# h_hi and h_lo computed directly from x and the gains, without a gained temporary, in a two-layer decoder trunk

## Chip, cores and metric

The kernel runs on one core of one Trainium2 chip. The metric is the device time of one execution in microseconds; shorter is better. The kernel before takes 2354.09 us, the median of 3 runs (2353.06 to 2355.17).

## What is computed

A trunk of two layers over 512 tokens of width 1024, all in float32. Each layer is half a SwiGLU block, a mixer with memory attention beside it, and another half SwiGLU block. Each part begins with an RMS norm. Cut to what matters:

```python
def rmsnorm(x, g):
    y = x * lax.rsqrt(jnp.mean(x * x, axis=-1, keepdims=True) + EPS)
    return y * g

for i in range(2):
    x = x + 0.5 * swiglu_ffn(rmsnorm(x, ffn1_norm[i]), ffn1_w_in[i], ffn1_w_out[i])
    h = rmsnorm(x, mix_norm[i])
    z = h @ w_in                                   # HGRN2 in layer 0, chunked gMLP in layer 1
    x = x + concat(mixer(z), memory_attention(z, mem_k, mem_v)) @ w_out
    x = x + 0.5 * swiglu_ffn(rmsnorm(x, ffn2_norm[i]), ffn2_w_in[i], ffn2_w_out[i])
return rmsnorm(x, final_norm)
```

## The kernel before, in words

x lies feature-major: 8 blocks of 128 features by 512 tokens. Every product of two float32 matrices is made of three TensorE (PE) matmuls: each operand is split into a high half, rounded to the type fp32r, and a low half, the operand less its high half. The PE computes high by high (L1093), high by low (L1094) and low by high (L1095). `unit` is one such product: one block of 128 output features, over 8 blocks of the contraction (24 matmuls of 512 columns) or, in the last third of an FFN's second matrix, over 6 (18 matmuls).

Weights come in units too. Four lanes of one buffer are used in turn. SyncE loads a lane (`raw`) once the PE is through with the unit that used it four units before; ScalarE (ACT) rounds it into `w_hi` (`hi`, L1528); VectorE (DVE) forms `w_lo` = raw - w_hi in place (`lo`, L1255). Both are issued two units ahead of the one being multiplied (`ahead`).

A phase is one weight matrix: first the memory's K and V for both layers (32 short units, "kv"), then for each layer `ffn_in`, `ffn_out`, the mixer's in and out, `ffn_in`, `ffn_out`. The last `ffn_out` is done by other code (`Final`).

Between phases stands h. In a phase whose name ends in `_out`, the four last units of each half give four new blocks of x. `take(g)` on DVE adds the PE's bank into x (L1478). Then, still in `take`, `gained` multiplies the block by the norm's gain, one value per partition, into a temporary (L1314); ACT's `h_top` rounds the temporary into `h_hi` (L1550); DVE's `h_rest` subtracts that from the temporary into `h_lo` (L1318). The factor 1/rms is applied later, to the results (`rstd`). GpSimd (POOL) squares each block of x (L1751) and adds it to a running sum (L1753). The first unit of the next phase reads h block by block and waits for each `h_lo`; behind it the PE multiplies the sum of squares by ones (L1159), from which DVE and ACT form `rstd` (L1363, L1586, L1365), which every later result needs.

In the kv phase the blocks of h for the first `ffn_in` are formed in the same three steps, one block per four units: `h_block` (the multiplication, DVE), `h_top` and `h_rest`. ACT also moves V out of PSUM there (`take_v`, L1560), and POOL stores it to DRAM (L1765).

Every engine works its queue strictly in the order of the code, so what stands ahead of an instruction in its queue can hold it. The order in the last four units (r == nr - 1) of an `_out` phase is, for step g:

```python
# DVE                                         # ACT
if g: take(g - 1)  # add, gained, h_rest      if g >= 1: take(g - 1)  # h_top
lo(next but one lane)                         hi(next but one lane)
# and after the four steps: take(3)
```

Of the kernel before, what the change touches and what calls it, by code (L numbers as in the profile page):

```python
# [30 lines left out]
ACT = mybir.ActivationFunctionType  # L31
# [5 lines left out]
DB = D // P  # L37
# [16 lines left out]
LANES = 4  # L54
# [30 lines left out]
def hybrid_trunk(nc, a, out):  # L85
# [34 lines left out]
    with ExitStack() as ctx:  # L120
# [5 lines left out]
        def sem(name):  # L126
            if name not in sems:
                sems[name] = ctx.enter_context(nc.semaphore(name))
            return sems[name]
# [50 lines left out]
        def f32(ap):  # L180
            return ap.bitcast(F32)
# [13 lines left out]
        def ahead(q, j):  # L195

            return (q, j + 2) if j + 2 < LANES else (q + 1, j - 2)

        def blocks_ahead(kind, r, g):

            rows = OUT_ROWS[kind]
            return rows[(r + (g >= 2)) % len(rows)][2]
# [2 lines left out]
        w_hi_ready, w_lo_ready = sem("w_hi_ready"), sem("w_lo_ready")  # L205
        unit_done = sem("unit_done")
        acc_read = sem("acc_read")
        xg_ready, h_hi_ready, h_lo_ready = sem("xg_ready"), sem("h_hi_ready"), sem("h_lo_ready")
        sq_ready, sq_sum_ready = sem("sq_ready"), sem("sq_sum_ready")
        ss_done, var_ready, std_ready, rstd_ready = (sem("ss_done"), sem("var_ready"), sem("std_ready"),  # L210
                                                     sem("rstd_ready"))
# [1040 lines left out]
        def _(dve):  # L1252
            def lo(q, j, nkb=KU):
                dve.wait_ge(w_hi_ready, LANES * q + j + 1)
                dve.tensor_tensor(lane_of(w_lo, q, j)[:, 0:nkb], lane_of(raw, q, j)[:, 0:nkb], f32(lane_of(w_hi, q, j)[:, 0:nkb]),  # L1255
                                  ALU.subtract).then_inc(w_lo_ready, 1)
# [51 lines left out]
                dve.tensor_scalar(small[:, 32:40], small[:, 24:32], -1.0, 1.0, ALU.mult, ALU.add).then_inc(sem("lb_step"), 1)  # L1308
                dve.wait_ge(sem("lb_step"), 7)

            def gained(s, m_, t):

                g = GAINS[s] + m_
                dve.tensor_scalar(t, x[:, m_, :], vecs[:, bass.ds(g, 1)], None, ALU.mult).then_inc(xg_ready, 1)  # L1314

            def h_rest(s, m_, t):
                dve.wait_ge(h_hi_ready, DB * s + m_ + 1)
                dve.tensor_tensor(h_lo[:, m_, :], t, f32(h_hi[:, m_, :]), ALU.subtract).then_inc(h_lo_ready, 1)  # L1318


            def kv_quad(it):
                first, turn = it == 0, kv_turn_of(it)

                def take(j):
                    if KV_QUADS[it] == "k":
                        dve.wait_ge(unit_done, LANES * it + j + 1)
                        if turn:
                            dve.wait_ge(sem(f"k_stored{j}"), 16 * turn)
                        dve.tensor_tensor(tmp[:, j, 0:MEM], acc[j][:, 0:MEM], rstd[:, 0:MEM], ALU.mult).then_inc(acc_read, 1)
                    if 2 <= LANES * it + j < DB + 2:  # L1330
                        take_x(LANES * it + j - 2)

                def h_block(m):
                    dve.wait_ge(sem("x_ready"), m + 1)
                    if m:
                        dve.wait_ge(h_lo_ready, m)
                    gained(0, m, tmp[:, 4, :])
                for j in range(LANES):
                    if first and j == 1:
                        lo(0, 3)  # L1340
                    if j:
                        take(j - 1)
                    if j == 1 and it:
                        h_block(it - 1)
                    if j == 2 and it:
                        h_rest(0, it - 1, tmp[:, 4, :])
                    if j == 2 and it == DB - 1:
                        h_block(it)
                    if j == 3 and it == DB - 1:
                        h_rest(0, it, tmp[:, 4, :])  # L1350
                    if not (first and j < 2):
                        lo(*ahead(it, j))
                take(3)
# [15 lines left out]
            for i, (kind, ph) in enumerate(phases):  # L1369
# [96 lines left out]
                elif ph is final.ph:  # L1466
                    final.vector(dve, lo)
                else:
                    rows = OUT_ROWS[kind]
                    nr = len(rows)  # L1470
                    scale = 0.5 if kind == "ffn_out" else 1.0
                    s += 1

                    def body(it, beside=None):
                        def take(g):
                            m_, t = LANES * it + g, tmp[:, 4 + g % 2, :]
                            dve.wait_ge(unit_done, LANES * (ph.q0 + nr * it + nr - 1) + g + 1)
                            dve.scalar_tensor_tensor(x[:, m_, :], acc[g][:], scale, x[:, m_, :], ALU.mult,  # L1478
                                                     ALU.add).then_inc(acc_read, 1)
                            dve.wait_ge(acc_read, ph.g0 + m_ + 1)  # L1480
                            gained(s, m_, t)
                            h_rest(s, m_, t)
                        for r in range(nr):
                            for g in range(LANES):
                                if beside:
                                    beside(LANES * r + g)
                                if r == nr - 1 and g:
                                    take(g - 1)
                                lo(*ahead(ph.q0 + nr * it + r, g), blocks_ahead(kind, r, g))
                        take(3)  # L1490
                    if kind == "hgrn_out":
                        hg = mixes[i - 1][1]

                        def beside(u):
                            if u < LANES:
                                hg.vector(dve, HEADS, u, False, True, True)
                            if u == LANES:
                                hg.vector(dve, HEADS + 1, 0, False, False, True)
                        body(0, beside)
                        body(1)  # L1500
                    elif kind == "gmlp_out":
                        gm = mixes[i - 1][1]

                        def beside(u):
                            if u < LANES:
                                gm.norm_vector(dve, 3, u)
                            if u == 0:
                                gm.u_vector(dve, 3, 3)
                                gm.mix_vector(dve, 2, 3)
                                gm.rest_vector(dve, 2, 3)  # L1510
                            if 1 <= u <= LANES:
                                gm.mix_vector(dve, 3, u - 1)
                                gm.rest_vector(dve, 3, u - 1)
                        body(0, beside)
                        body(1)
                    else:
                        loop(dve, 0, 2, body)
                        n_ffn += 1
# [3 lines left out]
        def _(act):  # L1522
# [22 lines left out]
            act.wait_ge(sem("mem_var"), 1)  # L1545
            act.activation(small[:, 60:62], small[:, 60:62], ACT.Sqrt).then_inc(sem("mem_std"), 1)

            def h_top(s, m_, t):
                act.wait_ge(xg_ready, DB * s + m_ + 1)
                act.activation(h_hi[:, m_, :], t, ACT.Copy).then_inc(h_hi_ready, 1)  # L1550

            def take_v(it, p):

# [9 lines left out]
            for it, kind in enumerate(KV_QUADS):  # L1563
                for j in range(LANES):
                    if it == 0 and j == 1:
                        hi(0, 3)
                    if it == 2 and j == 0:
                        act.wait_ge(sem("lb_shifted"), 3)
                        act.activation(small[:, 72:96], small[:, 72:96], ACT.Exp).then_inc(sem("lb_exp"), 1)
                        act.wait_ge(sem("mem_rstd"), 1)  # L1570
                    if j == 2 and it == DB - 1:
                        h_top(0, it, tmp[:, 4, :])
                    if j == 1:
                        if it:
                            h_top(0, it - 1, tmp[:, 4, :])
                        if it and KV_QUADS[it - 1] == "v":
                            take_v(it - 1, 1)
                    if j == 3 and kind == "v":
                        take_v(it, 0)
                    if not (it == 0 and j == 1):  # L1580
                        hi(*ahead(it, j))
# [7 lines left out]
            for i, (kind, ph) in enumerate(phases):  # L1589
# [85 lines left out]
                else:  # L1675
# [2 lines left out]

                    def body(it, beside=None):
                        def take(g):  # L1680
                            h_top(s, LANES * it + g, tmp[:, 4 + g % 2, :])
                        for r in range(nr):
                            for g in range(LANES):
                                if beside:
                                    beside(LANES * r + g)
                                if r == nr - 1 and g >= 1:
                                    take(g - 1)
                                hi(*ahead(ph.q0 + nr * it + r, g), blocks_ahead(kind, r, g))
                        take(3)
                    if kind == "hgrn_out":  # L1690
                        hg = mixes[i - 1][1]
# [151 lines left out]
```

## Time and profile before

| what | value |
|---|---|
| median of 3 runs | 2354.09 us |
| the profiled execution's own time | 2353.23 us |
| span of its trace | 2351.5 us |
| PE busy | 2328.8 us, 99% |
| DVE busy | 1233.5 us, 52% |
| ACT busy | 764.4 us, 33% |
| POOL busy | 264.5 us, 11% |
| PE's share of the chain that ended last | 92% |
| mean DMA rate | 100 GB/s |

The profile is of one execution. Its span runs from the first to the last instruction; 1.7 us of the execution's time lie around it. In the timeline the start of an instruction is given in us from the span's start, then its length; brackets show how long its engine had been idle and what released it. A matmul's length is modelled and overlaps the next one; the distance between starts is what a matmul costs.

### The profile page before, as it was taken

The numbers are of one execution on the slowest core, as the hardware profiler recorded it, in microseconds if no ns is written. First come the engines' busy times: TensorE is split into PE (matmuls) and PEld (weight loads), VectorE is DVE, ScalarE is ACT, GpSimd is POOL, SyncE is SP. The second block draws the span as 40 slices with busy tenths as digits, with TensorE's granted clock in tenths as the row PEclk, the third lists the DMA queues.
The fourth block names the chain that finished last, engine by engine and source line by source line (L and its number), as shares of the span: only waits on it lengthen the run. The fifth ranks groups of instructions, "written<-read, shape, count | busy, mean of one in ns | idle before, by whom it ended". The sixth has DMA issues, their size and how long they took to land.

```text
span 2351.5 us, 29800 instructions
## 1 busy us (share of the span) xinstructions
PE 2328.8 (99%) x11040; PEld 1947.6 (83%) x11040; DVE 1233.5 (52%) x1467; ACT 764.4 (33%) x1045; POOL 264.5 (11%) x236
## 2 busy tenths in 40 slices
PE   9999999999999999999999999999999999999998
PEld 9988888878888888888878888888888888888887
DVE  6654443467888654444445444336437644444422
ACT  4432222244445322222222222224433222222322
POOL 3400001111333420000110000120001212000000
PEclk9999999999999999999999999999999999999999
DMA  7733333332222333333333333333232233333322
GB/s 235 215 98 95 93 97 99 95 104 69 72 71 80 99 97 92 97 98 98 98 90 90 98 98 98 97 92 107 72 99 85 86 98 99 99 98 97 92 95 92
DMA packets 400693, 234.35 MB, mean 100 GB/s; under 512 B 7692, under 2 KB 386672, under 8 KB 400624
## 3 DMA queue, kind: packets, MB, share of 16 engines
q1 hardware_dynamic: 397328, 223.37, 32.1%
q0 software_dynamic: 3280, 10.02, 1.2%
q8 instruction: 47, 0.77, 0.1%
q14 instruction: 22, 0.18, 0.0%
q10 hardware_dynamic: 16, 0.00, 0.0%
HBM read 227.07 MB, written 6.29 MB: 99 GB/s over the span
## 4 chain that ended last, share of the span: by engine, by line
PE 92%; DVE 4%; ACT 2%; issue 1%; DMA 1%; POOL 0%; DVEq 0%; ACTq 0%; SPq 0%; POOLq 0%
PE acc L1093 26%; PE acc L1094 26%; PE acc L1095 26%; PE acc L847 1%; PE acc L846 1%; PE acc L848 1%; ACT w_hi L1528 1%; DVE w_lo L1255 1%; PE acc L262 1%; PE acc L264 1%; PE acc L263 1%; PE mix L264 1%; PE mix L262 1%; PE mix L263 1%; DMA raw<-in_mem_w_kv_dram 1%
## 5 line engine op out<-in xcount | busy, mean ns | idle before, releaser
L1255 DVE TENSOR_TENSOR w_lo<-raw,w_hi 128x1024 fp32r<-128x1024 f32 (+1 forms) x422 | 544.9, 1294 | 636.2 <-ACT w_hi L1528 623.1
L1093 PE MATMUL acc<-h_hi,w_hi 128*128 128x512 f32 x1920 | 756.0, 394 | 7.6 <-DVE h_lo L1318 5.3
L1094 PE MATMUL acc<-h_lo,w_hi 128*128 128x512 f32 x1920 | 748.5, 390 | 0.0
L1095 PE MATMUL acc<-h_hi,w_lo 128*128 128x512 f32 x1920 | 748.4, 390 | 0.0
L1528 ACT ACTIVATE w_hi<-raw 128x1024 fp32r<-128x1024 f32 (+1 forms) x422 | 436.4, 1038 | 341.7 <-DMA raw<-in_ffn_w_out_dram 219.6
L1093 PEld LDWEIGHTS acc<-h_hi,w_hi 128*128 128x128 f32 x1920 | 361.5, 188 | 84.4 <-DVE h_lo L1318 6.6
L1094 PEld LDWEIGHTS acc<-h_lo,w_hi 128*128 128x128 f32 x1920 | 361.5, 188 | 75.4 <-issue 2.0
L1095 PEld LDWEIGHTS acc<-h_hi,w_lo 128*128 128x128 f32 x1920 | 361.2, 188 | 75.4
L1093 PE MATMUL acc<-act_hi,w_hi 128*128 128x512 f32 (+1 forms) x976 | 367.6, 377 | 1.9 <-DVE w_lo L1255 1.2
L1095 PE MATMUL acc<-act_hi,w_lo 128*128 128x512 f32 (+1 forms) x976 | 365.7, 375 | 0.0
L1094 PE MATMUL acc<-act_lo,w_hi 128*128 128x512 f32 (+1 forms) x976 | 365.7, 375 | 0.0
L1381 DVE TENSOR_TENSOR tmp<-acc,rstd 128x512 f32<-128x512 f32 x176 | 121.7, 691 | 202.2 <-PE acc L1095 201.9
L1093 PEld LDWEIGHTS acc<-act_hi,w_hi 128*128 128x128 f32 x976 | 183.2, 188 | 36.0 <-DVE w_lo L1255 1.4
L1095 PEld LDWEIGHTS acc<-act_hi,w_lo 128*128 128x128 f32 x976 | 183.3, 188 | 33.2
L1094 PEld LDWEIGHTS acc<-act_lo,w_hi 128*128 128x128 f32 x976 | 183.5, 188 | 32.7
L1600 ACT ACTIVATE act_hi<-tmp 128x512 f32 (+1 forms) x88 | 55.6, 632 | 404.3 <-DVE tmp L1387 404.3
L1751 POOL TENSOR_TENSOR sq<-x 128x512 f32 (+1 forms) x48 | 57.6, 1201 | 1131.3 <-DVE x L1478 1130.7
L1596 ACT ACTIVATE tmp<-tmp 128x512 f32<-128x512 f32 x88 | 55.6, 632 | 255.5 <-DVE tmp L1381 255.5
L1550 ACT ACTIVATE h_hi<-tmp 128x512 fp32r<-128x512 f32 (+1 forms) x48 | 30.4, 632 | 200.7 <-DVE tmp L1314 200.7
L1392 DVE TENSOR_TENSOR act_lo<-tmp,act_hi 128x512 f32 (+1 forms) x88 | 60.6, 689 | 40.1 <-ACT act_hi L1600 40.1
L1753 POOL TENSOR_TENSOR sq<-sq 128x512 f32<-128x512 f32 x48 | 78.3, 1631 | 3.8
L1387 DVE TENSOR_TENSOR tmp<-tmp 128x512 f32<-128x512 f32 x88 | 60.9, 692 | 10.7
(243 smaller groups left out, 1895.0 us busy)
## 6 DMA issues: line engine op xcount, KB each, us to landing
raw<-in_ffn_w_in_dram SPq DMA_DIRECT2D x176, 512.0 KB, 3.7
raw<-in_ffn_w_out_dram SPq DMA_DIRECT2D x70, 512.0 KB, 3.4
raw<-in_hgrn_w_in_dram SPq DMA_DIRECT2D x40, 512.0 KB, 3.7
raw<-in_gmlp_w_in_dram SPq DMA_DIRECT2D x40, 512.0 KB, 3.6
raw<-in_mem_w_kv_dram SPq DMA_DIRECT2D x32, 512.0 KB, 4.4
raw<-in_gmlp_w_out_dram SPq DMA_DIRECT2D x24, 512.0 KB, 3.4
raw<-in_ffn_w_out_dram SPq DMA_DIRECT2D x24, 384.0 KB, 3.0
raw<-in_hgrn_w_out_dram SPq DMA_DIRECT2D x16, 512.0 KB, 3.4
```

Source lines behind the costliest of these rows:

```text
L1093: pe.matmul(bank, top[:, i, :], hi, start=(start and i == 0), stop=False)
L1094: pe.matmul(bank, top[:, i, :], lo, start=False, stop=False)
L1095: m = pe.matmul(bank, rest[:, i, :], hi, start=False, stop=(stop and i == last))
L1255: dve.tensor_tensor(lane_of(w_lo, q, j)[:, 0:nkb], lane_of(raw, q, j)[:, 0:nkb], f32(lane_of(w_hi, q, j)[:, 0:nkb]), ALU.subtract).then_in ...
L1381: dve.tensor_tensor(tmp[:, j, :], acc[j][:], rstd[:], ALU.mult).then_inc(acc_read, 1)
L1387: dve.tensor_tensor(tmp[:, j, :], tmp[:, j, :], tmp[:, j - 1, :], ALU.mult).then_inc(prod_done, 1)
L1392: dve.tensor_tensor(act_lo[:, f, :], tmp[:, j, :], f32(act_hi[:, f, :]), ALU.subtract).then_inc(act_lo_ready, 1)
L1528: act.activation(lane_of(w_hi, q, j)[:, 0:nkb], lane_of(raw, q, j)[:, 0:nkb], ACT.Copy).then_inc(w_hi_ready, 1)
L1596: act.activation(tmp[:, j, :], tmp[:, j, :], ACT.Silu).then_inc(silu_done, 1)
L1600: act.activation(act_hi[:, 2 * it + j // 2, :], tmp[:, j, :], ACT.Copy).then_inc(act_hi_ready, 1)
L1751: pool.tensor_tensor(sq_one, x[:, m_, :], x[:, m_, :], ALU.mult).then_inc(sq_ready, 1)
L1753: pool.tensor_tensor(sq_sum, sq_sum, sq_one, ALU.add).then_inc(sq_sum_ready, 1)
```

## The change

The multiplication by the gain into a temporary is removed with the semaphore `xg_ready`. ACT forms `h_hi` straight from x, with the gain as the activation's per-partition scale; DVE forms `h_lo` = x * gain - h_hi in one `scalar_tensor_tensor`. ACT's wait is now for x itself (`acc_read`, or `x_ready` in the kv phase). In the last four units of an `_out` phase the order on both engines changes: DVE adds into x, then splits the weights of the lane two ahead, then forms `h_lo`; ACT rounds those weights before it forms `h_hi`.

```diff
-            def gained(s, m_, t):
+            def h_rest(s, m_):
 
                 g = GAINS[s] + m_
-                dve.tensor_scalar(t, x[:, m_, :], vecs[:, bass.ds(g, 1)], None, ALU.mult).then_inc(xg_ready, 1)
-
-            def h_rest(s, m_, t):
                 dve.wait_ge(h_hi_ready, DB * s + m_ + 1)
-                dve.tensor_tensor(h_lo[:, m_, :], t, f32(h_hi[:, m_, :]), ALU.subtract).then_inc(h_lo_ready, 1)
-
+                dve.scalar_tensor_tensor(h_lo[:, m_, :], x[:, m_, :], vecs[:, bass.ds(g, 1)], f32(h_hi[:, m_, :]),
+                                         ALU.mult, ALU.subtract).then_inc(h_lo_ready, 1)
...
-                def h_block(m):
-                    dve.wait_ge(sem("x_ready"), m + 1)
-                    if m:
-                        dve.wait_ge(h_lo_ready, m)
-                    gained(0, m, tmp[:, 4, :])
...
-                    if j == 1 and it:
-                        h_block(it - 1)
                     if j == 2 and it:
-                        h_rest(0, it - 1, tmp[:, 4, :])
-                    if j == 2 and it == DB - 1:
-                        h_block(it)
+                        h_rest(0, it - 1)
                     if j == 3 and it == DB - 1:
-                        h_rest(0, it, tmp[:, 4, :])
+                        h_rest(0, it)
...
                         def take(g):
-                            m_, t = LANES * it + g, tmp[:, 4 + g % 2, :]
+                            m_ = LANES * it + g
...
-                            dve.wait_ge(acc_read, ph.g0 + m_ + 1)
-                            gained(s, m_, t)
-                            h_rest(s, m_, t)
...
                                 lo(*ahead(ph.q0 + nr * it + r, g), blocks_ahead(kind, r, g))
+                                if r == nr - 1 and g:
+                                    h_rest(s, LANES * it + g - 1)
                         take(3)
+                        h_rest(s, LANES * it + 3)
...
-            def h_top(s, m_, t):
-                act.wait_ge(xg_ready, DB * s + m_ + 1)
-                act.activation(h_hi[:, m_, :], t, ACT.Copy).then_inc(h_hi_ready, 1)
+            def h_top(s, m_, source, count):
+
+                g = GAINS[s] + m_
+                act.wait_ge(source, count)
+                act.activation(h_hi[:, m_, :], x[:, m_, :], ACT.Copy, scale=vecs[:, bass.ds(g, 1)]).then_inc(h_hi_ready, 1)
...
                     if j == 2 and it == DB - 1:
-                        h_top(0, it, tmp[:, 4, :])
+                        h_top(0, it, sem("x_ready"), it + 1)
                     if j == 1:
                         if it:
-                            h_top(0, it - 1, tmp[:, 4, :])
+                            if it == 1:
+                                act.wait_ge(sem("vecs_ready"), 2)
+                            h_top(0, it - 1, sem("x_ready"), it)
...
                         def take(g):
-                            h_top(s, LANES * it + g, tmp[:, 4 + g % 2, :])
+                            h_top(s, LANES * it + g, acc_read, ph.g0 + LANES * it + g + 1)
                         for r in range(nr):
                             for g in range(LANES):
                                 if beside:
                                     beside(LANES * r + g)
+                                hi(*ahead(ph.q0 + nr * it + r, g), blocks_ahead(kind, r, g))
                                 if r == nr - 1 and g >= 1:
                                     take(g - 1)
-                                hi(*ahead(ph.q0 + nr * it + r, g), blocks_ahead(kind, r, g))
                         take(3)
```

## Rows read from the trace of the kernel before

**Rows 1.** The page, part 1: busy us, share of the span, instructions
```profile
PE 2328.8 (99%) x11040; PEld 1947.6 (83%) x11040; DVE 1233.5 (52%) x1467; ACT 764.4 (33%) x1045; POOL 264.5 (11%) x236
```

**Rows 2.** The waits of PE: total us, times, longest
```profile
PE acc L1093 <- DVE h_lo L1318: 5.3, 3, 2.2
PE acc L1093 <- DVE w_lo L1255: 3.4, 4, 2.3
```

**Rows 3.** Timeline of PE at four of its idle stretches
```profile
70.96 0.36 PE L1093 MATMUL acc<-act_hi,w_hi 128*128 128x256 f32 x1 [0.36 <-DVE w_lo L1255]
...
109.81 0.77 PE L1093 MATMUL acc<-h_hi,w_hi 128*128 128x512 f32 x1 [2.27 <-DVE w_lo L1255]
...
1228.41 0.50 PE L1093 MATMUL acc<-h_hi,w_hi 128*128 128x512 f32 x1 [2.08 <-DVE h_lo L1318]
...
1591.32 0.50 PE L1093 MATMUL acc<-h_hi,w_hi 128*128 128x512 f32 x1 [1.05 <-DVE h_lo L1318]
...
1592.46 1.12 PE L1159 MATMUL mix<-sq,ones 128*128 128x512 f32 x2 [0.18 <-POOL sq L1753]
```

**Rows 4.** Timeline of PE at the end of layer 0's first ffn_out
```profile
471.46 0.39 PE L1093 MATMUL acc<-h_hi,w_hi 128*128 128x512 f32 x1
...
476.00 0.39 PE L1095 MATMUL acc<-h_hi,w_lo 128*128 128x512 f32 x1
478.60 0.79 PE L1093 MATMUL acc<-h_hi,w_hi 128*128 128x512 f32 x1 [2.21 <-DVE h_lo L1318]
```

**Rows 5.** Stretches: length, busy us by engine, granted PE clock, DMA share, GB/s
```profile
109.80:113.20 3.40, 3.39 (x8) 2.73 (x9) 1.50 (x2) 3.13 (x5) 2.71 (x4) 0.50 0.63 218
...
575.30:578.70 3.40, 1.41 (x12) 1.17 (x11) 2.64 (x3) 2.93 (x5) 2.17 (x2) 1.00 0.53 154
```

**Rows 6.** Timeline of DVE, same place as rows 4
```profile
469.58 0.68 DVE L1478 SCALAR_TENSOR_TENSOR x<-acc,x 128x512 f32 x1
470.41 1.37 DVE L1314 TENSOR_SCALAR tmp<-x,vecs 128x512 f32 x1
472.68 0.80 DVE L1318 TENSOR_TENSOR h_lo<-tmp,h_hi 128x512 f32 x1 [0.90 <-ACT h_hi L1550]
473.53 1.23 DVE L1255 TENSOR_TENSOR w_lo<-raw,w_hi 128x1024 fp32r<-128x1024 f32 x1
474.67 0.68 DVE L1478 SCALAR_TENSOR_TENSOR x<-acc,x 128x512 f32 x1
```

**Rows 7.** Timeline of POOL, same place
```profile
470.46 1.04 POOL L1751 TENSOR_TENSOR sq<-x 128x512 f32 x1 [2.62 <-DVE x L1478]
471.57 1.36 POOL L1753 TENSOR_TENSOR sq<-sq 128x512 f32<-128x512 f32 x1
```

**Rows 8.** Timeline of DVE, then POOL, near the end of kv
```profile
102.47 1.93 DVE L1255 TENSOR_TENSOR w_lo<-raw,w_hi 128x1024 fp32r<-128x1024 f32 x1 [2.37 <-ACT w_hi L1528]
104.32 1.77 DVE L1318 TENSOR_TENSOR h_lo<-tmp,h_hi 128x512 fp32r<-128x512 f32 x1
...
103.39 2.16 POOL L1753 TENSOR_TENSOR sq<-sq 128x512 f32<-128x512 f32 x1
```

**Rows 9.** Timeline of ACT, end of kv
```profile
106.72 0.63 ACT L1550 ACTIVATE h_hi<-tmp 128x512 fp32r<-128x512 f32 x1 [4.29 <-DVE tmp L1314]
...
109.87 0.83 ACT L1560 ACTIVATE tmp<-acc,small 128x256 f32<-128x256 f32 x2
```

**Rows 10.** Groups by form: busy us, mean ns, idle before
```profile
L861 ACT ACTIVATE work<-acc,small 128x512 f32<-128x512 f32 x16 | 10.8, 688 | 11.6 <-PE acc L848 11.6
```

**Rows 11.** Timeline of SyncE, and DMA issues of the page, part 6
```profile
463.72 0.37 SPq L973 DMA_DIRECT2D raw<-in_hgrn_w_in_dram  x1
...
raw<-in_hgrn_w_in_dram SPq DMA_DIRECT2D x40, 512.0 KB, 3.7
```

**Rows 12.** Timeline of DVE at the start of the first ffn_in
```profile
117.75 1.23 DVE L1255 TENSOR_TENSOR w_lo<-raw,w_hi 128x1024 fp32r<-128x1024 f32 x1 [6.46 <-DMA v_scratch<-tmp]
...
126.00 1.23 DVE L1255 TENSOR_TENSOR w_lo<-raw,w_hi 128x1024 fp32r<-128x1024 f32 x1 [1.65 <-ACT w_hi L1528]
```

More of the change, by code:

```diff
@@ L207, in hybrid_trunk @@
         acc_read = sem("acc_read")
-        xg_ready, h_hi_ready, h_lo_ready = sem("xg_ready"), sem("h_hi_ready"), sem("h_lo_ready")
+        h_hi_ready, h_lo_ready = sem("h_hi_ready"), sem("h_lo_ready")
         sq_ready, sq_sum_ready = sem("sq_ready"), sem("sq_sum_ready")
```

## The prediction

> **What bounds the kernel now.** The page comes first: the PE is busy 99% of the span, and DVE, ACT and POOL have room [rows 1]. A faster DVE is therefore worth nothing on average; only PE's idle time can be won. The list of PE's waits says how little that is: 5.3 us for `h_lo` in three places, 3.4 us for `w_lo` in four, the longest 2.3 [rows 2]. PE's timeline puts the long ones where phases meet. I call them A (end of kv, idle 2.27 us for `w_lo`), B (end of layer 0's first `ffn_out`, 2.21 for `h_lo`), C (layer 0's second, 2.08) and D (layer 1's first, 1.05) [rows 3, 4]. A fifth, G, is 0.36 us inside kv.
>
> Idle is not the whole price. In the 3.4 us after A the granted clock is 0.50, and the matmuls run at the 1.2 GHz level instead of 2.4; the same happens once after B and once after C (three stretches, one shown), but not after D, nor around 575 us, where the PE was idle for 2.0 us for another reason and the row shows 1.00 [rows 5]. Each such stretch costs half its length, 1.7 us.
>
> So between matmul starts, at 0.227 us each (471.46 to 476.00 are 20 steps), B lost 478.60 - 476.23 = 2.4 us, plus 1.7 for the clock. C lost 2.2 + 1.7. (A modelled end overlaps the next start, so the idle shown at B, 2.21, is 0.16 short of the loss; I add that at the others.) A lost 2.4 + 1.7. D lost 1.2 of idle, 0.3 in its slow restart (1592.46 - 1591.32 less three matmuls and the 0.18), and that 0.18 before the squares' matmul [rows 3, 4]. G lost 0.4. Altogether 14.2 us, 0.6% of the kernel. That is the ceiling.
>
> **Why B, C and D stall.** The last units of `ffn_out` have 18 matmuls, 4.1 us. DVE's step from one add to the next is 474.67 - 469.58 = 5.1 us [rows 6]: add 0.7, gain 1.4, wait for ACT 0.9, `h_lo` 0.8, `w_lo` 1.2. It falls 1 us behind per unit. The fourth unit's result exists at about 471.7 (the next unit starts at 471.46 [rows 4]), but its add starts at 474.67 and `h_lo` comes 3.9 us later, at 478.5. The PE needs that block 21 matmuls after 471.46, at 476.2. `hgrn_out` and `gmlp_out` end in units of 24 matmuls, 5.4 us, more than DVE's 5.1, and no stall shows there.
>
> **The parts of the change.**
>
> Removed: 48 gain multiplications. Alone one takes 0.49 us, but beside POOL's square (470.46 to 471.50) it took 1.37 and ended 0.3 after POOL did [rows 6, 7]: a blocked instruction. That part of 1.4 us per step goes, with the wait of 0.15 before it, and with it the semaphore hop to ACT.
>
> Added on ACT: a scale read from a column. The trace has it in L861, 0.69 us from PSUM [rows 10]; without it `h_hi` takes 0.63 [rows 9]. I take 0.63 and keep 0.69 as the other end; it is hidden behind DVE's `w_lo` either way.
>
> Added on DVE: `h_lo` as scalar_tensor_tensor with two SBUF tensors. The nearest rows are L1478 with one operand in PSUM, 0.68, and the subtraction it replaces, 0.69 to 0.80 [rows 6]. I take 0.7. The upper end is 1.77, that subtraction beside POOL at 104.32 [rows 8].
>
> This upper end matters, since the removed instruction leaves two-tensor instructions alone beside POOL. At 102 to 106 us they alternate: `w_lo` 1.93, POOL's add 2.16 instead of 1.36, `h_lo` 1.77, each waiting for the one before [rows 7, 8]. The Trainium skill, "SBUF — State Buffer", section "Who interferes with whom", has a rule for it: a DVE instruction with two SBUF inputs and a GpSimd instruction that reads SBUF exclude each other for their whole length, and whoever comes first wins. By that rule, the trace agrees at 104.32, and a fused `h_lo` can be blocked no less than the old one. Without any blocking a step would be 0.7 + 1.2 + 0.7 = 2.6 us.
>
> I reckon the blocking in. x is ready at T + 0.7. In the new order `w_lo` is next in DVE's queue, if `w_hi` is there; POOL wakes 0.2 us later (469.58 + 0.68 against 470.46 [rows 6, 7]), so `w_lo` should win: 1.2, then POOL's square 1.04, then `h_lo` 0.7. Step: 3.6 us, under 4.1. ACT forms `h_hi` meanwhile. If POOL wins every time: 0.85 + 1.04 + 1.1 + 1.36 + 0.7 = 5.0, hardly better than now.
>
> Is `w_hi` there? ACT now rounds the weights ahead of `h_hi`. The lane for step 3 is asked for at 463.72 and lands 3.7 later, at 467.4 [rows 11]; rounding takes at most 1.2, as the same block's `w_lo` [rows 6], so 468.5 or so, and that step's add ends at 467.8 + 0.7 = 468.5. It is a close race in steps 2 and 3 and clear in step 1. With one race lost, lag is below 1 us: add 471.9 to 473.4 at worst, `h_lo` of the last block 474.3 to 475.2. Needed: 476.2. The stall is gone, and with the idle the slow clock. What is late next? The sum of squares: POOL's square and add follow the last x and end near 475.5 to 476.5, and the PE asks at 471.46 + 5.45 = 476.9. It fits, narrowly. Gain: B 4.1, C 3.9, D 1.7.
>
> A. ACT's `h_hi` of the last block stands ahead of the rounding of the lane that A waits for, and was itself idle 4.29 us for the gain multiplication, which stood behind the two blocked DVE instructions [rows 8, 9]. Now it needs only x, long ready. That lane is asked for when the last kv unit but three is done. Kv's last units have 256 columns, so 2.8 us each, half of 5.4; PE's idle began at 109.81 - 2.27 = 107.5 [rows 3], so the load starts near 99. It lands 3.7 later [rows 11], is rounded by 104 and has its `w_lo` by 105.3, before the PE's 107.4. But another chain follows: `w_lo` of the third `ffn_in` unit waits for V's last store (6.46 us idle), and the fourth unit's ends at 126.00 + 1.23 = 127.2 [rows 12]. The store begins after `take_v`, at 109.87 [rows 9], held by ACT's queue; now its unit is done at 107.5 and it can start at 107.6, so this chain moves forward only 2.2 us, to 125.0. The PE, 2.4 us earlier and at full clock, wants that fourth unit at 107.4 + 3 x 5.45 + 0.9 = 124.6 (0.9 is L1159, 1.12 less its overlap [rows 3]). New stall 0.4 to 0.5 us. Gain of A: 4.1 - 0.5 = 3.6.
>
> G. `w_lo` came late through the same ACT queue: 0.4.
>
> Sum: 4.1 + 3.9 + 1.7 + 3.6 + 0.4 = 13.7 us. The profiled execution took 2353.23 (span 2351.5 and 1.7 around it), giving 2339.5; the median of the runs is 0.9 higher, giving 2340.4.
>
> Costed at nothing: the changed order in the first halves of the `_out` phases and in `hgrn_out` and `gmlp_out`. Its cover is the PE's 5.4 us per unit against a step of at most 5.0; without that cover it would cost up to 0.5 us in each of two places.
>
> **Rivals.**
>
> *POOL wins the races.* Steps of 5.0 us leave the last add 2.7 us late at 474.6; `h_lo` then takes 0.7 + 1.2 + 0.7 and ends at 477.2, a stall of 1.0. For it: the gain multiplication lost that race at 470.41 by 0.05 us. Against: `w_lo` does not wait for the add. B and C keep 1.0 each, D keeps most of 1.2; one idle microsecond brought no slow clock at D. Gain 13.7 - 3.2 = 10.5, or 7.1 if the clock falls all the same: 2344 to 2347.
>
> *The clock or A takes some back.* The idle stretch at 575 us is 2.0 long and stays; C's was 2.08 and did lower the clock. Falling there or at the fourth unit of A costs 1.7 each: 2342 to 2344.
>
> *A new wait takes the old one's place.* The PE waits for the sum of squares instead of `h_lo`, since POOL is the loser of the races that DVE wins. Three squares and adds, each delayed by 1.2, would end the sum 2 us late, and the slow clock stays: 2350 to 2354, no change. Against it: POOL works 2.4 of 4.1 us per unit.
>
> *Slower: a late weight load now holds h.* ACT's queue puts `h_hi` behind a DMA. After the landing, rounding, `h_hi`, a blocked wait and `h_lo` take 3.8 us, so block 6 is there at 471.3 and needed at 475.5. From a load of 8 us upwards each us is a us of PE time, and beyond 10.5 us the place is worse than before. To be slower by over 0.2% it would take loads of about 12 us at B, C and D together. The row's 3.7 speaks against it.
>
> **How the numbers follow.** Forecast 0.60; POOL wins 0.13; clock or A 0.13; new wait 0.09; slower 0.05. Predicted time 2340.4. The forecast's own range is 2338 to 2342.5 (the ceiling of 14.2, the spread of the runs, the half microseconds of A and of the races). To leave out no more than 2 in 10 the range takes in the next two cases: 2337.5 to 2347. A change of under 0.2% (4.7 us) can't be told from none here: faster 0.86, same 0.09, slower 0.05.
>
> **What would show it.** PE's waits: `h_lo` gone or under 1 us, `w_lo` under 1 us; the granted clock 1.00 behind A, B and C; starts of the adds at the end of `ffn_out` 4.1 us apart; `h_lo` lengths between 0.7 and 1.8; at A a new wait at the fourth `ffn_in` unit. I am wrong if the adds stay 5 us apart, if L1159 waits for POOL by over 1 us, or if a slow stretch of the clock turns up elsewhere.

## The result: 14.9 us faster, and the profile after

The changed kernel takes 2339.16 us, the median of 5 runs (2338.49 to 2340.8), against 2354.09 before (5 runs, 2352.48 to 2355.17). The ratio is 0.9938, with a 95% interval of 0.9925 to 0.9952. The forecast was 2340.4.

The profiled execution took 2339.09 us with a span of 2337.3, 14.2 less than before. The first part of its page, and then the list of PE's waits (total us, times, longest; two of 0.3 and 0.2 left out), answer to [rows 1, 2]:

```profile
PE 2321.8 (99%) x11040; PEld 1944.8 (83%) x11040; DVE 1207.4 (52%) x1419; ACT 772.6 (33%) x1045; POOL 278.2 (12%) x236
```

```profile
PE mix L580 <- POOL work L767: 2.0, 1, 2.0
PE acc L1051 <- POOL small L1716: 1.9, 1, 1.9
PE acc L1093 <- DVE act_lo L1267: 1.8, 1, 1.8
PE mix L455 <- DVE act_hi L418: 1.6, 1, 1.6
PE acc L1137 <- DVE w_lo L1255: 0.3, 1, 0.3
```

The 5.3 us for `h_lo` are gone altogether. Of the 3.4 for `w_lo`, A (2.3) and G (0.4) are gone, and 0.3 came new in another place. The remaining 0.8 were two waits at 14.6 and 18.4 us, at the kernel's start, which the change doesn't touch. DVE has 48 instructions less.

What still holds the PE lies elsewhere. The 1.8 us for `act_lo` stand at the kernel's start, at 11 us, and were 0.5 in the profile before. The PE was through with its transposes 1.0 us earlier than before, and what it waits for came 0.3 us later. Behind this wait the granted clock was 0.51 for 3.4 us, a slow stretch that the profile before does not have (1.00 there in the same stretch):

```profile
11.07 0.36 PE L1093 MATMUL acc<-act_hi,w_hi 128*128 128x256 f32 x1 [1.83 <-DVE act_lo L1267]
...
12.10:15.50 3.40, 3.40 (x18) 3.40 (x17) 2.77 (x5) 3.37 (x6) 0.00 (x0) 0.51 1.02 420
```

It cost nothing that lasted: matmul for matmul, the changed kernel was 0.8 us behind the one before at 16 us and level with it at 35 us.

Set side by side matmul by matmul, the two traces drift apart for good in four places: 4.1 us at A, 4.1 at B, 3.9 at C, 1.7 at D. The remaining 0.3 lies before A. The timeline of DVE in the changed kernel, at the place of [rows 6], shows how:

```profile
459.19 0.69 DVE L1466 SCALAR_TENSOR_TENSOR x<-acc,x 128x512 f32 x1 [1.07 <-PE acc L1095]
459.91 1.23 DVE L1255 TENSOR_TENSOR w_lo<-raw,w_hi 128x1024 fp32r<-128x1024 f32 x1
461.05 1.53 DVE L1315 SCALAR_TENSOR_TENSOR h_lo<-x,vecs,h_hi  x1
463.27 0.69 DVE L1466 SCALAR_TENSOR_TENSOR x<-acc,x 128x512 f32 x1 [0.70 <-PE acc L1095]
464.10 1.23 DVE L1255 TENSOR_TENSOR w_lo<-raw,w_hi 128x1024 fp32r<-128x1024 f32 x1
465.24 1.53 DVE L1315 SCALAR_TENSOR_TENSOR h_lo<-x,vecs,h_hi  x1
467.36 0.69 DVE L1466 SCALAR_TENSOR_TENSOR x<-acc,x 128x512 f32 x1 [0.58 <-PE acc L1095]
469.18 0.75 DVE L1315 SCALAR_TENSOR_TENSOR h_lo<-x,vecs,h_hi  x1 [1.13 <-ACT h_hi L1540]
```

The adds start 4.1 us apart instead of 5.1, and before each DVE is idle, waiting for the PE: it is the PE that sets the pace. POOL's timeline at the same place, with the last two matmul groups of PE behind it:

```profile
464.16 2.07 POOL L1743 TENSOR_TENSOR sq<-x 128x512 f32 x1 [0.43 <-DVE x L1466]
466.30 1.62 POOL L1745 TENSOR_TENSOR sq<-sq 128x512 f32<-128x512 f32 x1
468.24 1.04 POOL L1743 TENSOR_TENSOR sq<-x 128x512 f32 x1 [0.31 <-DVE x L1466]
469.36 1.72 POOL L1745 TENSOR_TENSOR sq<-sq 128x512 f32<-128x512 f32 x1
```

```profile
467.03 0.39 PE L1093 MATMUL acc<-h_hi,w_hi 128*128 128x512 f32 x1
...
472.24 0.40 PE L1095 MATMUL acc<-h_hi,w_lo 128*128 128x512 f32 x1
472.47 1.02 PE L1159 MATMUL mix<-sq,ones 128*128 128x512 f32 x2
```

The blocking has changed sides ("blocked" means here that an instruction has started but ends only some time after another engine's). POOL's square, alone 1.04 us, takes 2.07 where `w_lo` was first; `h_lo` then waits for the square and takes 1.53 instead of 0.75. The last `h_lo` ends at 469.93; the PE would want it 21 matmuls after 467.03, at 471.8. The sum of squares is ready at 471.1, wanted at 472.5.

At C it went less smoothly. DVE's timeline and, behind it, POOL's:

```profile
1205.19 0.69 DVE L1466 SCALAR_TENSOR_TENSOR x<-acc,x 128x512 f32 x1 [1.07 <-PE acc L1095]
1206.16 2.04 DVE L1255 TENSOR_TENSOR w_lo<-raw,w_hi 128x1024 fp32r<-128x1024 f32 x1 [0.28 <-ACT w_hi L1516]
1208.12 1.78 DVE L1315 SCALAR_TENSOR_TENSOR h_lo<-x,vecs,h_hi  x1
1209.82 0.68 DVE L1466 SCALAR_TENSOR_TENSOR x<-acc,x 128x512 f32 x1
```

```profile
1206.07 1.04 POOL L1743 TENSOR_TENSOR sq<-x 128x512 f32 x1 [0.81 <-DVE x L1466]
```

`w_hi` came late, POOL's square began 0.1 us before `w_lo`, and the step took 4.6 us. The next one took 3.5, and DVE was waiting for the PE again. One lost step of 4.6 is covered.

The stretches behind A and around B of the changed kernel (length, busy us by engine, granted clock, DMA share, GB/s) answer to [rows 5]:

```profile
107.10:113.50 6.40, 6.40 (x29) 4.95 (x28) 1.23 (x1) 3.83 (x5) 3.40 (x4) 1.00 0.68 213
467.00:474.00 7.00, 7.00 (x30) 5.45 (x29) 4.08 (x4) 2.96 (x3) 6.02 (x6) 1.00 0.38 104
```

The PE is busy throughout at a granted clock of 1.00.

### The profile page after: what moved, and what is told of

Read it like the earlier page. It is cut to its first block, busy times and chain, and to the rows that moved or that the text cites. A ratio compares the mean times of both kernels' runs of the same rounds, so it can differ in the third digit from the quotient of the medians.

```text
span 2337.3 us, 29722 instructions
## 1 busy us (share of the span) xinstructions
PE 2321.8 (99%) x11040; PEld 1944.8 (83%) x11040; DVE 1207.4 (52%) x1419; ACT 772.6 (33%) x1045; POOL 278.2 (12%) x236
## 4 chain that ended last, share of the span: by engine, by line
PE 94%; DVE 3%; ACT 1%; POOL 0%; DMA 0%; issue 0%; SPq 0%; ACTq 0%; DVEq 0%; POOLq 0%
PE acc L1093 26%; PE acc L1095 26%; PE acc L1094 26%; PE acc L846 1%; PE acc L848 1%; PE acc L847 1%; PE acc L262 1%; PE acc L264 1%; PE acc L263 1%; PE mix L263 1%; PE mix L262 1%; PE mix L264 1%; DVE w_lo L1255 1%; PE acc L1137 1%; PE mix L913 1%; PE acc L1138 1%
## 5 line engine op out<-in xcount | busy, mean ns | idle before, releaser
L1255 DVE TENSOR_TENSOR w_lo<-raw,w_hi 128x1024 fp32r<-128x1024 f32 (+1 forms) x422 | 534.8, 1269 | 643.7 <-ACT w_hi L1516 632.6
L1743 POOL TENSOR_TENSOR sq<-x 128x512 f32 (+1 forms) x48 | 70.5, 1469 | 1106.7 <-DVE x L1466 1105.1
L1466 DVE SCALAR_TENSOR_TENSOR x<-acc,x 128x512 f32 (+1 forms) x40 | 27.6, 691 | 79.6 <-PE acc L1095 79.6
```

The costliest lines, as they stand in the source:

```text
L1743: pool.tensor_tensor(sq_one, x[:, m_, :], x[:, m_, :], ALU.mult).then_inc(sq_ready, 1)
```

## The experiments

The rival theories were these: the stalls went because DVE has one instruction less, blocked or not; because POOL no longer stretches it; or because of the new order, which fills the wait for ACT with other work. And, for the size of the gain, whether the slow clock belongs to each stall.

**One phase at a time.** `kv_only` takes from the change what stands in the kv phase, `out_only` the rest.

```diff
# kv_only: h_block and its gained() removed; for layer 0's first ffn_in
-  h_top(0, it - 1, tmp[:, 4, :])
+  h_top_x(0, it - 1, sem("x_ready"), it)
-  h_rest(0, it - 1, tmp[:, 4, :])
+  h_rest_x(0, it - 1)
# out_only: the same two functions, and the new order, in the _out phases alone
```

> The change in the kv phase alone; all _out phases as before. Theory (the gain multiplication and ACT's queue held the first ffn_in's weights; 2.4 us of idle plus 1.7 of slow clock): 4.2 us faster than before, about 2350; C, B and D keep their 4.1, 3.9 and 1.7. Rival (the gain came from the order in the _out phases only, and A moved with chance): no difference beyond 1 us.

> The change in the _out phases alone; kv as before. Theory: 9.7 us faster than before, about 2344.5, A keeps its idle of 2.3 us and the slow clock behind it. Rival (the parts are not additive, one slow stretch of the clock moves elsewhere): 7 to 8 us, with a slow stretch at a new place.

Measured: `kv_only` 2346.86 us (7 runs), ratio 0.997 (0.9959 to 0.9981), 6.9 us under the 2353.8 of before on the same chip; `out_only` 2345.78 (5 runs), ratio 0.9964 (0.995 to 0.9977), 8.0 us. Both parts help and their sum, 14.9, is what the whole gives. But the division is not the expected 4.2 and 9.7. In `kv_only`'s trace A is gone, C is as before, and B kept its idle, but no slow stretch lies behind it. That missing stretch is 1.7 us of gain which the edit did not aim at. In `out_only`'s trace A kept its 2.27 us of idle, without a slow stretch; one lies behind the stall at 572 us instead, which had none before. That the two gains add up to the whole is therefore partly luck: each depends on which of the stalls left in it brought a slow stretch.

**Fusion without the order.**

```diff
# fuse_only: the changed kernel, last four units
-  lo(next but one lane)
   if r == nr - 1 and g: h_rest(s, LANES * it + g - 1)
+  lo(next but one lane)
# and on ACT
-  hi(next but one lane)
   if r == nr - 1 and g >= 1: take(g - 1)      # h_top
+  hi(next but one lane)
```

> h_hi and h_lo from x as in the changed kernel, everywhere, but with the old order in the last four units: DVE add, h_lo, weights; ACT h_hi ahead of the weights. Theory (blocking by POOL counts, order does the rest): a step of 4.1 to 5.0 us, the add of the fourth unit up to 2.7 us late, a stall of 0 to 1 us at each ffn_out; 2339 to 2345. Rival (the removed instruction alone is enough): step 4.1, no stall, 2339, the same as the changed kernel.

Measured: 2340.02 us (2339.47 to 2341.65), ratio 0.994 (0.9927 to 0.9954): within 1 us of the changed kernel. The step, though, is not 4.1. DVE's timeline in `fuse_only`:

```profile
465.10 0.68 DVE L1466 SCALAR_TENSOR_TENSOR x<-acc,x 128x512 f32 x1
466.90 0.75 DVE L1315 SCALAR_TENSOR_TENSOR h_lo<-x,vecs,h_hi  x1 [1.13 <-ACT h_hi L1540]
467.72 2.17 DVE L1255 TENSOR_TENSOR w_lo<-raw,w_hi 128x1024 fp32r<-128x1024 f32 x1
469.81 0.68 DVE L1466 SCALAR_TENSOR_TENSOR x<-acc,x 128x512 f32 x1
```

It is 4.7 us, DVE still lags behind the PE, and waits 1.1 us for ACT in every step. The lag just fits into the cover that the next phase's first unit gives `h_lo`. What no longer fits is the sum of squares. Its last add on POOL and PE's L1159 in `fuse_only`:

```profile
471.80 1.72 POOL L1745 TENSOR_TENSOR sq<-sq 128x512 f32<-128x512 f32 x1
```

```profile
473.03 0.39 PE L1095 MATMUL acc<-h_hi,w_lo 128*128 128x512 f32 x1
473.57 1.13 PE L1159 MATMUL mix<-sq,ones 128*128 128x512 f32 x2
```

The add ends at 473.52 and L1159 starts at 473.57, 0.54 after the matmul before it instead of 0.23. That is 0.3 us, and 0.35 to 0.4 in all at each of B, C and D: about 1.1 us, the size of the difference between the two medians, but smaller than what these runs can tell apart.

**Order without the fusion.**

```diff
# order_only: the kernel before, last four units
   take(g - 1)       # add and gained, without h_rest
   lo(next but one lane)
+  h_rest(s, LANES * it + g - 1, tmp[:, 4 + (g - 1) % 2, :])
# and on ACT hi() ahead of h_top()
```

> Before, with only the new order in the last four units of the _out phases: DVE add, gain multiplication, weights, h_lo; ACT weights ahead of h_hi. kv as before. Theory (the wait of 0.9 us for ACT is filled with the weights' split, the gain multiplication stays blocked at 1.4): step 4.1 to 4.5 us, B, C and D mostly gone, 2345 to 2349. Rival (only the removed instruction helps): adds stay 5 us apart, 2354.

Measured: 2350.43 us (11 runs, 2349.04 to 2353.74), ratio 0.9988 (0.9979 to 0.9997): 3.4 us faster, less than my theory had. DVE's timeline:

```profile
465.14 1.37 DVE L1314 TENSOR_SCALAR tmp<-x,vecs 128x512 f32 x1
466.43 2.31 DVE L1255 TENSOR_TENSOR w_lo<-raw,w_hi 128x1024 fp32r<-128x1024 f32 x1
468.66 0.68 DVE L1318 TENSOR_TENSOR h_lo<-tmp,h_hi 128x512 f32 x1
469.26 0.68 DVE L1478 SCALAR_TENSOR_TENSOR x<-acc,x 128x512 f32 x1
```

```profile
466.30 1.36 POOL L1755 TENSOR_TENSOR sq<-sq 128x512 f32<-128x512 f32 x1
```

The wait of 0.9 for ACT is filled, but `w_lo` now meets POOL's add (the second fence), which used to run beside that wait, and takes 2.31 instead of 1.23. The adds stay 4.95 us apart; B keeps 1.79 us of idle. I had forgotten that an empty stretch of DVE was where POOL worked unhindered.

The 3.4 us overstate what the order does. PE's waits for `h_lo` fell only from 5.3 to 4.0 us. The larger part of the 3.8 us between the two profiled executions is the clock: this trace has a slow stretch behind B alone, so two fewer than before, 3.4 us. One of the two is A's, where the idle is 2.28 us and the edit changes nothing.

**Which engine's order.**

```diff
# fuse_act_order: the changed kernel with DVE's old order and ACT's new one
-  lo(next but one lane)
   if r == nr - 1 and g: h_rest(s, LANES * it + g - 1)
+  lo(next but one lane)
```

> The changed kernel with DVE's old order (add, h_lo, weights) and ACT's new one (weights ahead of h_hi). Theory: DVE's h_lo now waits for ACT, which rounds weights first when they land late; the order on DVE matters, step 4.5 to 5, 2340 to 2345. Rival (ACT's order is what matters): as the changed kernel, 2339.

Measured: 2340.72 us (2338.59 to 2341.44), ratio 0.9946 (0.9932 to 0.9959). Its step is 4.7 us like `fuse_only`'s, and it keeps the same 0.4 us at B, C and D. So what little the order gives comes from DVE's side; ACT's alone gives nothing that the trace shows. The medians can't tell these kernels apart, and DVE's new order with ACT's old one was not tried.

**Without POOL's work.** The same edit in the kernel before and in the changed one:

```diff
-  pool.tensor_tensor(sq_one, x[:, m_, :], x[:, m_, :], ALU.mult).then_inc(sq_ready, 1)
-  pool.wait_ge(sq_ready, DB * s + m_ + 1)
-  pool.tensor_tensor(sq_sum, sq_sum, sq_one, ALU.add).then_inc(sq_sum_ready, 1)
+  pool.sem_inc(sq_ready, 1)            # in the _out phases only
+  pool.sem_inc(sq_sum_ready, 1)
```

> Before, with POOL's squares and adds of the _out phases left out (only semaphores are raised; the sum is a constant, so the later norms are not computed). If POOL's use of SBUF is what stretches DVE's instructions: the gain multiplication takes 0.49 us everywhere, h_lo 0.69, a step is 4.1 to 4.2 us, and B, C and D vanish: about 2344.5. If the stretch has another cause, or the number of instructions alone counts: steps stay at 5.1 and the time at 2354.

> The changed kernel with the same work left out. If blocking by POOL is hidden in the changed order: h_lo takes 0.74 us in the _out phases instead of 1.5, and the time stays at 2339 within 1 us. If POOL still costs PE time somewhere: faster by more than 1 us.

Measured: 2345.02 us for before (ratio 0.9964, 0.995 to 0.9977) and 2341.05 for the changed one (0.9945, 0.9931 to 0.9959; 2339.03 to 2341.41). In the first, every gain multiplication takes 0.49 us. DVE's timeline of it, a step of 4.2:

```profile
465.39 0.69 DVE L1478 SCALAR_TENSOR_TENSOR x<-acc,x 128x512 f32 x1
466.23 0.49 DVE L1314 TENSOR_SCALAR tmp<-x,vecs 128x512 f32 x1
467.63 0.69 DVE L1318 TENSOR_TENSOR h_lo<-tmp,h_hi 128x512 f32 x1 [0.91 <-ACT h_hi L1550]
468.47 1.22 DVE L1255 TENSOR_TENSOR w_lo<-raw,w_hi 128x1024 fp32r<-128x1024 f32 x1 [0.15 <-ACT w_hi L1528]
```

B, C and D vanish with nothing of the change made. So POOL's square and add were what made the gain multiplication dear, and removing either them or it is enough. In the changed kernel `h_lo` falls from a median of 1.44 to 0.75 us and the time does not fall: there the blocking is covered. (Its median is even 1.9 us above the changed kernel's, which ran at another time; the two profiled executions, 2339.31 and 2339.09, are 0.2 apart.)

**The clock.** Since the slow stretches had not stayed with their stalls, the kernel before was profiled twice more, and the two halves of the change once more each.

> The kernel before once more, for a second profile. If the slow clock follows each idle stretch of over 2.05 us by rule: stretches at A, B and C again, none at 575. If it is partly chance: another set of places, and a time that differs by 1.7 us for each one more or less, with the idle stretches themselves the same.

> The kernel before, a third profile. By rule: slow stretches of the clock behind A, B and C, none at 575, as in the first. By chance: another set, the idle stretches the same.

> The change in the kv phase alone, a second profile. Its first had 2.3 us of idle at B and no slow stretch there, but one at C. By rule: the same again. By chance: another set.

> The change in the _out phases alone, a second profile. Its first had A's idle of 2.4 us without a slow stretch, and one behind the 2.0 us at 570. By rule: the same again. By chance: another set.

Measured, one execution each: 2352.84, 2356.54, 2347.69 and 2345.66 us. PE's idle at C in `before_again` and in `before_third`, and the stretches around it (the clock is the figure in front of the last two):

```profile
1229.63 0.50 PE L1093 MATMUL acc<-h_hi,w_hi 128*128 128x512 f32 x1 [2.08 <-DVE h_lo L1318]
...
1227.00:1235.00 8.00, 5.92 (x25) 4.21 (x24) 5.71 (x5) 4.77 (x5) 2.48 (x3) 1.00 0.24 66
```

```profile
1231.77 0.50 PE L1093 MATMUL acc<-h_hi,w_hi 128*128 128x512 f32 x1 [2.08 <-DVE h_lo L1318]
...
580.20:583.60 3.40, 3.40 (x13) 2.92 (x12) 3.23 (x3) 2.56 (x4) 1.29 (x1) 0.51 0.02 6
1229.00:1237.00 8.00, 5.92 (x18) 3.75 (x17) 4.55 (x5) 4.31 (x5) 2.61 (x3) 0.79 0.22 66
```

The row from 580.20 lies behind the stall of 2.0 us near 575 us. The idle stretches repeat to 0.02 us; the slow ones do not. 2.08 us of idle at C brought none in `before_again` and one in the other two profiles; the 2.0 us at 575, which I had taken for harmless, brought one in `before_third`. A and B had one in all three profiles of before. Yet A had none in the two of `out_only` and in that of `order_only`, with the same 2.27 or 2.28 us, and B none in the two of `kv_only`, with 2.06, but one in `order_only`, with 1.79. The 2.0 us near 575, which every kernel here keeps, brought one in 5 of all 14 profiles (one of each run in this document). Whether a stall is followed by the 1.2 GHz level is thus partly chance, and seems to depend on what went before; on what, these runs do not settle.

Times go with it: of the 17 executions of the kernel before beside `kv_only`, the fastest (2349.7 us) had a mean granted clock of 0.999 and the slowest (2356.56) 0.996.

**One step on.** The list of waits after the change names 1.6 us for the first head's K (L418). Splitting it one unit earlier:

```diff
-  if s in (2, 3, 5, 7):
+  if s in (1, 3, 5, 7):
       yield "k", (s - 1) // 2
```

> The changed kernel with the first head's K split one unit earlier (step 1 instead of 2) in both attention stages. Theory: the PE's wait of 1.6 us for that split at 484 us shrinks to 0.2 to 0.5, and the smaller one in layer 1 too: 1.2 to 2 us faster than the changed kernel, about 2337.5. Rival: K's load lands too late for step 1, or the queue only shifts the wait to the second query block: no gain.

Measured: 2337.14 us (2336.8 to 2339.66), ratio to before 0.9933 (0.9919 to 0.9946), 2.0 us under the changed kernel's median, which ran at another time; its interval overlaps the changed kernel's. The trace decides better. The wait in the changed kernel, and in `k_early`:

```profile
486.01 0.39 PE L455 MATMUL mix<-act_hi,act_lo 128*128 128x256 f32 x1 [1.60 <-DVE act_hi L418]
```

```profile
484.53 0.35 PE L455 MATMUL mix<-act_hi,act_lo 128*128 128x256 f32 x1 [0.21 <-DVE act_hi L479]
```

It is 1.4 us shorter, and the PE now waits for the query's low half. In layer 1 the PE's wait of 0.2 us at the same place is gone too.

## Why the prediction was right, and where it was not

*The ceiling.* Only PE's idle at the seams could be won: shown. 13.7 us were forecast, 14.2 came in the trace and 14.9 in the medians. The forecast of 2340.4 is 1.2 off.

*B, C, D.* 4.1, 3.9 and 1.7 us were forecast, and 4.1, 3.9 and 1.7 came. At B and D the chain behind it held link by link: `w_lo` won the races, POOL's square came between, `h_lo` was blocked, and the step was below the PE's. The last `h_lo` ended 2.9 us after the next phase's first matmul (467.03), within the 2.8 to 3.7 that the forecast had after 471.46; the sum of squares was ready 1.4 us before it was wanted, the good end of my 0.4 to 1.4 (these figures are B's). At C `w_lo` lost one race, the case that the forecast allowed for, and the lag of that step was made up in the next.

*Blocking by POOL.* Shown by leaving POOL's work out. The upper end of 1.77 us for a blocked `h_lo` held: its longest was 1.78.

*The two new instructions.* `h_lo` takes 0.75 us unblocked where I took 0.7. ACT's `h_hi` with its scale takes 0.72, not the 0.63 that I chose: my upper end was the better row [rows 10]. Neither shows in the time.

*A.* Forecast 3.6 us, came 4.1. The step that failed is the new stall of 0.4 to 0.5 us at the fourth unit of `ffn_in`. I let the DMA of V's last store take as long as before. DVE's row in the changed kernel, and its second one further on, answer to [rows 12]:

```profile
113.80 1.23 DVE L1255 TENSOR_TENSOR w_lo<-raw,w_hi 128x1024 fp32r<-128x1024 f32 x1 [4.79 <-DMA v_scratch<-tmp]
...
122.05 1.23 DVE L1255 TENSOR_TENSOR w_lo<-raw,w_hi 128x1024 fp32r<-128x1024 f32 x1 [1.65 <-ACT w_hi L1516]
```

The store was issued 2.2 us earlier, as forecast (111.59 against 113.82 in POOL's timelines), but DVE was released 2.2 us after that instead of 3.9. The fourth unit's `w_lo` ended at 123.3, not 125.0, and no wait followed. It was not the change that made the store land faster. In `before_again`, the kernel before, POOL issues it and DVE is released:

```profile
115.71 0.58 POOL L1765 DMA_DIRECT2D v_scratch<-tmp  x1
...
117.92 1.23 DVE L1255 TENSOR_TENSOR w_lo<-raw,w_hi 128x1024 fp32r<-128x1024 f32 x1 [4.72 <-DMA v_scratch<-tmp]
```

That is 2.2 us too, and `before_third` and seven of the other ten profiles have the same; one has 2.5, and `order_only` and `out_only_again` have 3.7. The forecast took 3.9 us from a single execution. Why a store takes longer in some executions stays open. Without the new stall A gives back its whole 4.1.

*G.* 0.4 us forecast; the wait at 71 us is gone, but one of 0.3 came at 87. By the start of A the changed kernel was 0.3 us ahead. Between profiles of the kernel before that point alone differs by 2 us, so nothing can be made of it.

*The slow clock.* Its size was right, its rule wrong. I gave every long stall at A, B and C its own 1.7 us as if it had to come. For the whole change that does no harm, since all three stalls went; for a part it does, and the stretch missing behind B is 1.7 of the 2.7 us by which `kv_only` beat its expected 4.2. The other 1.0 stays open. There was luck in the size too. The profile from which I reckoned had three such stretches at the seams; `before_again` has two, and from it the same reckoning would have given 1.7 us less. I also named a slow stretch elsewhere as a sign that I was wrong. One did turn up, at 12 us, but behind a wait at the start, in code that the change leaves alone, and it cost nothing that lasted. (The profiles of `fuse_only` and `after_no_squares` have it too, behind waits of 2.0 and 1.9 us; the other eleven, with at most 1.2 there, do not.)

*The rivals.* The new wait for the sum of squares is real without the new order on DVE, worth 0.3 to 0.4 us at each seam; with that order it does not come. The step of 4.7 us that comes without that order costs 1.1 us in all, a third of the 3.2 that I gave the case of 5.0. The rival that the clock takes some back at the stall of 2.0 us did not come in this profile (the clock was 1.00 there), but that stall stays, and it brought a slow stretch in 5 of 14 profiles. The part of the change that I worked out at most length, the order, matters least: fusion alone gives 13.8 of the 14.9 us.

## What to carry to other kernels

When a helper engine falls behind only for a few units at a seam, compare its step with the bound engine's there, not its busy share: 5.1 us against 4.1 was the whole case, and an edit that brings the step near enough takes the stall away. Here 4.7 us was near enough and 4.95 was not. Before filling an engine's wait with other work, look which other engine worked unhindered during that wait. And price a stall by its idle time, with the slow clock behind it as a chance beside it, read from several profiles. A landing time, too, should come from more than one profile: the one term that failed here was a single store's.

## What the runs showed of the hardware that was not expected

- The same idle of the PE, 2.08 us at the same place of the same kernel, is followed by a stretch of 3.4 us at a granted clock of 0.50 in two executions of three. A stall of 2.0 us was followed by one in 5 of 14 profiles, one of 1.79 us in the single profile that has it.
- A one-input DVE multiplication from SBUF to SBUF is held by POOL as well as the two-input instructions are: 0.49 us alone, 1.37 beside POOL's square.
- ScalarE's copy of 128x512 from SBUF takes 0.63 us, and 0.72 with a per-partition scale read from SBUF.
- From the issue of V's last store on POOL to the release of the DVE instruction behind it, 11 of 14 profiles have 2.2 to 2.5 us and three 3.7 to 3.9, across kernels.
